# Replacing TensorE transposes by VectorE block transposes and SBUF-to-SBUF transfers in a float32 decoder block

## What is computed

```
x = x + 0.5 * ((silu(h @ w_gate1) * (h @ w_up1)) @ w_down1)     h = rms_norm(x)     w_gate, w_up: 2048 x 5632
b, c, xv, q, k, v = split(rms_norm(x) @ w_in)                                        w_in: 2048 x 6144
y_conv = b * causal_depthwise_conv(c * xv, 3 taps)
a = softmax(q1 k1^T) - lam * softmax(q2 k2^T)                   8 heads, two score maps of width 64 each
y_attn = 0.8 * rms_norm(a @ v)
x = x + concat(y_conv, y_attn) @ w_out                                               w_out: 2048 x 2048
x = x + 0.5 * swiglu(rms_norm(x)) with a second set of weights
return rms_norm(x)
```

## Time and profile before

| | |
|---|---|
| runs, us | 1841.43 median of 3 (1840.94 to 1841.82) |
| the profiled execution | 1841.93 us, of which the span is 1839.6 |
| PE busy | 1827.1 us, 99% |
| DVE, ACT, POOL busy | 1123.5 us (61%), 834.9 us (45%), 26.5 us (1%) |
| granted TensorE clock | 0.999 |
| DMA | 350.17 MB, 190 GB/s, SP's queue 61.5% of 16 engines |

### The profile page before, as it was taken

How to read it: one execution, slowest core, us unless ns; L and a number is a source line. 1 busy time by engine, 2 the same in 40 slices (tenths; PEclk the granted TensorE clock), 3 DMA queues, 4 the chain that set the end, 5 groups by cost and what they waited for, 6 DMA issues and landing times.

```text
span 1839.6 us, 23353 instructions
## 1 busy us (share of the span) xinstructions
PE 1827.1 (99%) x8201; PEld 1509.9 (82%) x8201; DVE 1123.5 (61%) x1497; ACT 834.9 (45%) x996; POOL 26.5 (1%) x36
## 2 busy tenths in 40 slices
PE   9999999999999999999999999999999999999998
PEld 7888888888888888888888888888888888888886
DVE  6666666666655554557647755666666666654554
ACT  6444444444444444455445445444444444443443
POOL 0000000000000000000000000000000000000000
PEclk9999999999999999999999999999999999999999
DMA  7666666666655556655664556666666666655554
GB/s 256 194 194 194 194 193 190 193 190 192 193 195 194 186 191 194 208 171 167 189 182 152 184 186 189 194 193 194 193 192 193 190 191 193 194 194 195 195 194 137
DMA packets 181451, 350.17 MB, mean 190 GB/s; under 512 B 10896, under 2 KB 11536, under 8 KB 181264
## 3 DMA queue, kind: packets, MB, share of 16 engines
q1 hardware_dynamic: 180672, 347.65, 61.5%
q0 software_dynamic: 144, 1.05, 0.2%
q10 hardware_dynamic: 576, 0.69, 0.1%
HBM read 347.25 MB, written 2.10 MB: 190 GB/s over the span
## 4 chain that ended last, share of the span: by engine, by line
PE 99%; DMA 1%; SPq 0%; issue 0%; ACT 0%; DVE 0%; DVEq 0%; ACTq 0%
PE bank L314 32%; PE bank L316 32%; PE bank L315 32%; PE bank L352 1%; DMA x<-in_x_dram 1%; PE bank L454 0%; PE bank L471 0%; PE bank L440 0%; PE bank L462 0%; PE bank L371 0%; PE bank L479 0%; SPq L244 0%; ACT x L583 0%; DVE yT_lo L939 0%; ACT w_hi L550 0%
## 5 line engine op out<-in xcount | busy, mean ns | idle before, releaser
L764 DVE TENSOR_TENSOR w_lo<-raw,w_hi 128x1024 fp32r<-128x1024 f32 x655 | 809.0, 1236 | 676.0 <-ACT w_hi L550 674.0
L550 ACT ACTIVATE w_hi<-raw 128x1024 fp32r<-128x1024 f32 x655 | 693.6, 1059 | 875.8 <-PE bank L316 870.9
L314 PE MATMUL bank<-w_hi,xT_hi 128*128 128x512 f32 x1788 | 699.5, 391 | 0.0
L316 PE MATMUL bank<-w_hi,xT_lo 128*128 128x512 f32 x1788 | 696.1, 389 | 0.0
L315 PE MATMUL bank<-w_lo,xT_hi 128*128 128x512 f32 x1788 | 695.7, 389 | 0.0
L314 PEld LDWEIGHTS bank<-w_hi,xT_hi 128*128 128x128 f32 x1788 | 335.7, 188 | 71.4 <-issue 2.7
L316 PEld LDWEIGHTS bank<-w_hi,xT_lo 128*128 128x128 f32 x1788 | 335.6, 188 | 70.2
L315 PEld LDWEIGHTS bank<-w_lo,xT_hi 128*128 128x128 f32 x1788 | 335.8, 188 | 68.6
L314 PE MATMUL bank<-w_hi,hT_hi 128*128 128x512 f32 x704 | 274.1, 389 | 0.0
L316 PE MATMUL bank<-w_hi,hT_lo 128*128 128x512 f32 x704 | 273.9, 389 | 0.0
L315 PE MATMUL bank<-w_lo,hT_hi 128*128 128x512 f32 x704 | 273.9, 389 | 0.0
(11 more groups left out here) (115 smaller groups left out, 428.2 us busy)
## 6 DMA issues: line engine op xcount, KB each, us to landing
raw<-in_ffn_w_up_dram SPq DMA_DIRECT2D x176, 512.0 KB, 4.0
raw<-in_ffn_w_down_dram SPq DMA_DIRECT2D x176, 512.0 KB, 3.6
raw<-in_ffn_w_gate_dram SPq DMA_DIRECT2D x175, 512.0 KB, 4.4
raw<-in_w_in_dram SPq DMA_DIRECT2D x96, 512.0 KB, 4.1
raw<-in_w_out_dram SPq DMA_DIRECT2D x32, 512.0 KB, 3.6
x<-in_x_dram SPq DMA_DIRECT2D x3, 512.0 KB, 9.6
out_dram<-x SPq DMA_DIRECT2D x6, 256.0 KB, 2.4
gfin<-in_final_norm_dram POOLq DMA_DIRECT2D x1, 1024.0 KB, 5.2
```

What stands on the lines that cost most here:

```text
L314: pe.matmul(acc, hi[:, kt, ts], w_hi[slot][:, kk], start=(k == 0 and kk == 0), stop=False)
L316: mm = pe.matmul(acc, lo[:, kt, ts], w_hi[slot][:, kk], start=False, stop=(k == chunks - 1 and kk == KC - 1))
L550: act.activation(w_hi[slot][:], raw[slot][:], ACT.Copy).then_inc(hi_ready, 1)
L764: dve.tensor_tensor(w_lo[slot][:], raw[slot][:], w_hi[slot][:].bitcast(F32), ALU.subtract)\
```

## The change

FFN hidden groups, residual blocks and the parts Q, K, B are turned in two steps. First, two STREAM_TRANSPOSEs over all 128 partitions (`turn_quads`), one per token tile, turn every 32 x 32 block where it stands and sort the blocks by target quadrant, into `gate` (seen as `mid`). Then 16 transfers from SBUF to SBUF (`move`: four calls of four transfers, 32 partitions by 256 elements, 32 KB each) put every block on its partitions: into `turn_in` itself for hidden groups and blocks, into `q_quads`, `kT`, `bT` for the parts. They are issued by SP between the weight loads, four after each of four loads. ACT and DVE then split from `turn_in` instead of from `gate` or PSUM, with patterns that walk runs of 32 elements; for hidden groups at steps 6 and 7 instead of 4 and 5, for blocks at step 6 (w_out) or 14 (down) instead of 1. DVE splits a block in 8 pieces instead of 4. Scores read `qT` (one ACT copy per half) and `kT` directly. The last block of each residual, C, the heads and the attention matrix stay on PE. ACT's squares write their unused result to PSUM or `head` instead of `gate`. SP's loops for the down, mixer and w_out loads are unrolled.

The diff, cut to its core:

```diff
+            def move(q, to, done):
+
+                for j in range(QUADS):
+                    sp.dma_start(to[32 * j:32 * j + 32, q].rearrange("r k t i -> r (k t i)"),
+                                 mid[32 * q:32 * q + 32, j].rearrange("r k t i -> r (k t i)")).then_inc(done, 16)
+
+            def move_hidden(f, c, q):
+
+                if q == 0:
+                    sp.wait_ge(hid_turned, f * GROUPS + c)
+                move(q, turned_in, hid_moved[f])
+
+            def move_block(n, q, squared):
+
+                if q == 0:
+                    sp.wait_ge(block_turned, n)
+                    sp.wait_ge(squares_ready, squared)
+                    sp.wait_ge(x_saved, n + 1 + n // XG)
+                move(q, turned_in, block_moved)
+
+            def move_part(n, q, to):
+
+                if q == 0:
+                    sp.wait_ge(part_turned, n)
+                move(q, to, part_moved)
...
                         load(base + 2 * CD * c + CD * u + k, k % RING, w, k, c * W)
+                        if u == 1 and k < QUADS and not first:
+                            move_hidden(f, c, k)
+                        if u == 0 and k < QUADS and first and f == 1:
+                            move_block(2 * (XG - 1), k, 3 * XG - 1)
...
+            def after_down(f):
+                def after(g, k):
+                    if g == 0 and 8 <= k < 8 + QUADS:
+                        move_hidden(f, GROUPS, k - 8)
+                    if g > 0 and 8 <= k < 8 + QUADS and f == 0:
+                        move_block(g, k - 8, XG + g)
+                return after
+
+            def after_out(g, k):
+                if g >= 2 and k < QUADS:
+                    move_block(XG - 1 + g - 1, k, 2 * XG + g - 1)
...
+                        load(CH_MIX + 6 * CD * j + CD * u + k, k % RING, w_in, k, j * W + PART[u])
+                        if u == V and k < QUADS:
+                            move_part(3 * j + 1, k, q_quads)
+                        if u == B and k < QUADS:
+                            move_part(3 * j + 2, k, kT)
+                        if u == X and k < QUADS:
+                            move_part(3 * j + 3, k, bT)
+            down(CH_OUT, w_out, CD, OUT_ORDER, after_out)
...
                             if k == 0 and second == 0 and i == 0 and early:
                                 early()
-                            if k == 1 and (second or i) and not final:
-                                turn_drained(tb + 4 * i + 2 * second - 2, pr + i + second - 1, 1 - second)
...
-            def turn_qk(hb, tb, pair, h):
+            def scores(hb, h, j):
 
                 if h == 0:
-                    for d in drained:
-                        pe.wait_ge(d, (pair + 1) * TT)
+                    pe.wait_ge(part_moved, MOVED * (3 * j + 2))
+                    pe.wait_ge(q_copied, j + 1)
+                    pe.wait_ge(conv_copied, 2 * j)
                 else:
-                    pe.wait_ge(turned_lo, tb + h - 1)
-                for n, u in enumerate((Q, K)):
-                    for t in range(TT):
-                        mm = pe.transpose(bank[4][:, n * SEQ + t * P:n * SEQ + (t + 1) * P],
-                                          part_s[u][:, t, h * DV:(h + 1) * DV], ident[:])
-                mm.then_inc(qk_turned, 1)
-
-            def scores(hb, h, jb):
-
-                pe.wait_ge(qk_copied, hb + h + 1)
-                if h > 0:
                     pe.wait_ge(masked, hb + h)
-                if h == HJ - 1:
-                    pe.wait_ge(conv_copied, jb + 2)
                 for c in range(2):
                     cs = slice(c * DK, (c + 1) * DK)
                     for t in range(TT):
                         mm = pe.matmul(bank[5 + c][:, t * P:t * P + (t + 1) * P],
-                                       qkT[cs, t * P:(t + 1) * P], qkT[cs, SEQ:SEQ + (t + 1) * P],
+                                       qT[cs, h, t * P:(t + 1) * P], kT[cs, :, h, 0:t + 1].rearrange("p q t i -> p t q i"),
                                        start=True, stop=True)
...
             def split_hidden(hid, c):
-                act.wait_ge(hid_turned, hid + c + 1)
-                act.activation(hT_hi[:, bass.ds(BT * c, BT), :], hidT, ACT.Copy).then_inc(hid_hi, 1)
+                act.wait_ge(hid_moved[hid // GROUPS], MOVED * (c + 1))
+                act.activation(by_quads(hT_hi[:, bass.ds(BT * c, BT), :]), by_rows(turned_in), ACT.Copy).then_inc(hid_hi, 1)
...
+            def split_block(r, g):
 
                 act.wait_ge(gcol_ready, r + g + 1)
-                split_x(tb + 2 * g, T_HIGH, gcol, xT_hi, BT * g)
+                act.wait_ge(block_moved, MOVED * (r * (XG - 1) // XG + g + 1))
+                for b in range(BT):
+                    a = act.activation(xT_hi[:, BT * g + b].rearrange("p (t q i) -> p t q i", t=TT, q=QUADS),
+                                       turned_in[:, :, b].rearrange("p q t i -> p t q i"), ACT.Copy, scale=gcol[:, b:b + 1])
+                    if b % 2:
+                        a.then_inc(turned_hi, 1)
...
-            def turn_hidden(i):
-
-                src = turn_in[:].rearrange("p t (b q c) -> p t b q c", b=BT, q=4)
-                dst = hidT.rearrange("p b (t q c) -> p t b q c", t=TT, q=4)
-                for j in range(4):
-                    v = dve.transpose(dst[32 * j:32 * j + 32, :, :, i], src[32 * i:32 * i + 32, :, :, j])
-                if i == 3:
-                    v.then_inc(hid_turned, 1)
+            def turn_quads(src, done):
+
+                for t in range(TT):
+                    v = dve.transpose(mid[:, :, :, t].rearrange("p j k i -> p k j i"),
+                                      src[:, t].rearrange("p (k j i) -> p k j i", k=BT, j=QUADS))
+                v.then_inc(done, 1)
...
-                dve.tensor_tensor(hT_lo[:, tiles, :], hidT, hT_hi[:, tiles, :].bitcast(F32), ALU.subtract)\
-                   .then_inc(hid_lo, 1)
+                dve.tensor_tensor(by_quads(hT_lo[:, tiles, :]), by_rows(turned_in), by_quads(hT_hi[:, tiles, :]).bitcast(F32),
+                                  ALU.subtract).then_inc(hid_lo, 1)
...
+            def split_block(tb, g):
+
+                for b in range(BT):
+                    if b % 2 == 0:
+                        dve.wait_ge(turned_hi, tb + 2 * g + b // 2 + 1)
+                    for t in range(TT):
+                        ts = slice(t * P, (t + 1) * P)
+                        v = dve.scalar_tensor_tensor(
+                            out=xT_lo[:, BT * g + b, ts].rearrange("p (q i) -> p q i", q=QUADS), in0=turned_in[:, :, b, t],
+                            scalar=gcol[:, b:b + 1], op0=ALU.mult, op1=ALU.subtract,
+                            in1=xT_hi[:, BT * g + b, ts].bitcast(F32).rearrange("p (q i) -> p q i", q=QUADS))
+                    if b % 2:
+                        v.then_inc(turned_lo, 1)
...
                             if k == chunks - 1:
                                 dve.wait_ge(squares_ready, q + g)
                                 dve.wait_ge(x_saved, r + g + 1)
+                                if g > 0 and not final:
+                                    dve.wait_ge(turned_lo, tb + 2 * g)
...
-                            if k == 1 and g > 0 and not final:
-                                split_drained(tb, g - 1)
+                            if k == 0 and g > 0 and not final:
+                                dve.wait_ge(drained[1 - second], (pr + (g - 1) // 2 + 1) * TT)
+                                turn_quads(turn_in, block_turned)
+                            if k == (6 if chunks == CD else 14) and g > 0 and not final:
+                                split_block(tb, g - 1)
...
+                        if u in (K, V, C) and k == 0:
+                            n = (K, V, C).index(u)
+                            dve.wait_ge(drained[(u - 1) % 2], (pair + (u - 1) // 2 + 1) * TT)
+                            if 3 * j + n > 0:
+                                dve.wait_ge(part_moved, MOVED * (3 * j + n))
+                            turn_quads(part_s[u - 1], part_turned)
```

More of the change, by code:

```diff
@@ L34 @@
 P = 128
+QUADS = 4
+MOVED = 16 * QUADS * QUADS
 D = 2048
@@ L265, in first_chunk, with down @@
                 sp.dma_start(raw[0][:, 1], src[:, 1, 0:W]).then_inc(raw_loaded[0], 16)
[L267 to L272, removed]
+            def down(base, w, chunks, order, after=None):
+                for g in range(XG):
+                    for k in range(chunks):
+                        load(base + chunks * g + k, (chunks * g + k) % RING, w, order[k], g * W)
+                        if after:
+                            after(g, k)
             first_chunk(wg1)
@@ L280, in _ @@
             load_x(3)
-            gate_up(CH_FFN1, wg1, wu1, 0, opened=RING)
+            def after_down(f):
[8 more added lines that the diff above has]
+                    move_block(XG - 1 + g - 1, k, 2 * XG + g - 1)
+            gate_up(0, CH_FFN1, wg1, wu1, 0, opened=RING, first=True)
             with sp.Fori(1, GROUPS) as c:
```

(27 more changed lines are left out.)

107 lines of the change are left out of this document (55 added, 52 removed).

## The result

| | median, us | range | runs |
|---|---|---|---|
| before | 1841.45 | 1840.94 to 1841.82 | 4 |
| changed | 1830.78 | 1830.46 to 1831.22 | 4 |

The ratio is 0.9942 (95% interval 0.993 to 0.9955): faster by 10.7 us. The forecast was 1830.8.

What follows compares the result with a forecast made beforehand. PE's own instruction list was taken as the bound: 1841.93 for the profiled execution less 10.5 and 0.1 gives 1831.3, and 1830.8 as median, 0.5 lower. Forecast 1829.5 to 1833.5 (0.78); 8 in 10: 1829.3 to 1838.

Steps and rivals of the forecast that it cites:

- 96 transposes, 10.5 us: PE loses 48 transposes at residual blocks, 32 at heads, 16 at B; by distance of starts, 0.109 us each, 10.5 us.
- Small terms: On PE: narrower starts behind removed transposes gain 0.1 us; scores reading K in runs, stall at last convolution, squares: 0.
- Rivals 1 and 2: Scores pay for K's runs, 1834 to 1838, 0.08; transfers collide with PE's SBUF reads, 1839 to 1852, 0.08 (full, shared).
- The tight place in w_out: At w_out blocks, moved data land by 16 to 16.4 us, ACT wants them at 17.4; least room in the program.
- room of 2.9 us: In w_out, the `low` of step 7 is ready at 24.3 us and PE needs it at 27.2.
- the rooms: Slack behind PE: 5.8 us for DVE's low part, 4.4 for the load; a load costs nothing until some 10.2 late.
- rival 3's threshold: SP's queue becomes the bound: PE stalls each site from 1.22 us per issue; at 1.3, 1875; 0.08 shared, in full.
- its bound of 1.06 us: Dearest SP issue on record, at the start; at that price the next load is 7.6 us late, still under 10.2.

## Why the prediction was right

- **What bounds it.** PE's list: shown by the two halves of the change (all the gain with the 96 transposes, none with 125 us less of DVE).
- **96 transposes, 10.5 us.** 10.65 in the chain, 10.7 in the medians, and 0.1125 each where they were added by themselves. The 275 ns of the Trainium skill (TensorE: Matmul & The Clock Gate, PE-mode transpose), there the length of one within another kernel, would by estimate have made it 26 us; the runs do not show that price between matmuls of this kind.
- **Small terms.** Scores with K in runs of 32 cost 0.86 as before; the stall at the last convolution stayed; the starts in FFN 1 did not widen. Rivals 1 and 2 have nothing.
- **DVE.** 0.687 a transpose for 0.7; its busy time 107.5 us lower, about 100 was said.
- **DMA engines.** A share of 0.79 in the chunks of a site, for 0.83. The transfers landed 2.6 us after issue and were issued 0.6 us apart, so they overlapped, as the prediction had it. The 2.0 us that it quotes from the Trainium skill (DMA: Bandwidth & Descriptors, Anatomy of one DMA) is given there for transfers issued by GpSimd, and these are SP's; 16 of them one after another would be 32 us, not 34. Neither is a term of the sum.
- **The tight place in w_out.** The data were to be there 1 us before ACT's split. It waited 0.20, 0.74 and 1.49 us, and PE nothing: of the room of 2.9 us behind it half was used at the last block.
- **SP: the term that was mis-sized.** The prediction took 0.373 us per issue, by the row of a load that SP issues after a wait. An issue that follows another at once took 0.59 (0.51 the first of a run); so did the loads between, 0.58 in w_out. A step was 3.0 to 3.2 us and not 1.9: SP did not keep up, and the forecast stood on the rooms.
- **The rooms, and rival 3's threshold, were wrong too.** By the prediction PE should have stalled from 1.22 us per issue on. Two issues of 0.617 in place of one are 1.23, and cost 6.4 us per site. ACT's place in the order (split of step 6 ahead of the rounding of step 7) and the scores' need of K come before the load's route does. Where the edge lies between 0.59 and 1.23 was not measured. An estimate for the hidden groups: 16 issues, each dearer by 0.64, let the rounding slip 9.9 us where 5.8 are free, so the edge is near 0.59 + 0.64 x 5.8 / 9.9 = 0.97. In w_out, with 1.4 of 2.9 us left and 16 issues, it is nearer still, near 0.7. The forecast held because 0.59 stays inside all of them.
- **Luck.** That the sum met the median to 0.1 us is luck: the runs of one kernel scatter by 0.8. That an issue dearer by more than half would cost nothing, the prediction had said by its bound of 1.06 us; but by the estimate above that bound already lies beyond the edge, so it was right about 0.59 through rooms larger than the real ones.

## What to carry to other kernels

Price an instruction on a pipelined engine by the distance of starts, and read the gain of a removal from that engine alone: as long as the others wait for it, what they gain is worth nothing. When transfers are put on a queue between loads, price their issue by back-to-back ones, and follow every consumer of the moved data in its own engine's order, not only the loads behind them. A short stall of another engine's making is worth looking for beside a large change: here one edit of a step gave about a seventh of what the whole change gave.

## What was not expected of the hardware

- Issues of SP back to back took 0.59 us for 32 rows and 0.59 for 16 (0.617 a piece with the space between), while a load of 512 KB after a wait took 0.37: the number of rows did not matter, the neighbour did. Why is open; issues from another queue were not tried.
- Behind a wait of 4 us PE's granted clock was at its lower level while seven matmuls started 0.42 us and more apart, and the cost of the stalls grew by half (75 us beside 143). Behind the changed kernel's gap at 1031.05 one start stood 0.33 us off, the next ones 0.23, and the granted clock stayed at 1.00.
- The length of a gap alone did not tell whether the clock falls. With Q, K and B in two pieces PE's starts stood 2.3 us too far apart at 787.18 and again at 873.50, and PE had been busy without a pause for 4 us ahead of both. Behind the first the clock stayed at 1.00, behind the second it was 0.72 in the mean of 2.5 us (columns as above):

```profile
787.00:790.00 3.00, 2.82 (x12) 2.36 (x13) 2.74 (x5) 2.33 (x3) 0.00 (x0) 1.00 0.84 274
873.50:876.00 2.50, 2.50 (x10) 2.10 (x11) 2.50 (x3) 1.66 (x3) 0.00 (x0) 0.72 0.36 95
```
